# Layer norms: totals over partitions as columns of a product with one column of ones

## The reference

```
x <- LayerNorm(ALPHA * x + gate * sublayer(x * (1 + scale) + shift))

def layer_norm(x, g, b):
    mu = xf.mean(-1, keepdims=True)
    var = jnp.square(xf - mu).mean(-1, keepdims=True)
    return ((xf - mu) * lax.rsqrt(var + LN_EPS) * g + b)
```

## Time and profile before

| | |
|---|---|
| median of 3 runs | 3970.11 us |
| the profiled execution | 3970.7 us |
| its span | 3968.9 us |
| mean granted TensorE clock | 0.954 |
| TensorE busy | 3631.7 us (92%) |
| DVE busy | 2469.6 us (62%) |
| ACT busy | 937.8 us (24%) |
| POOL busy | 1844.6 us (46%) |

### The profile page before, as it was taken

The page is one execution under the profiler, slowest core; times in us unless marked ns, Lnnn a source line. Parts: engine busy times, 40 slices in busy tenths (PEclk is TensorE's granted clock), DMA queues, the critical chain, the costliest instruction groups (busy, mean ns, idle before and its releaser), DMA issues.

```text
span 3968.9 us, 74547 instructions
## 1 busy us (share of the span) xinstructions
PE 3631.7 (92%) x31532; PEld 3416.5 (86%) x31532; DVE 2469.6 (62%) x3517; ACT 937.8 (24%) x1804; POOL 1844.6 (46%) x875
## 2 busy tenths in 40 slices
PE   8999999999889778888999994899999989999998
PEld 3877799999778678888999994799998777899997
DVE  5366678758784456655885668886677556632125
ACT  5422231001243245542310012300013322220011
POOL 1310146656355645535566552366554201356663
PEclk9999999999999888999999997899999999999999
DMA  8100024333234443322343331244332000122221
GB/s 317 62 12 17 17 81 149 133 117 122 68 136 170 142 88 93 84 54 95 106 144 126 124 101 40 80 138 138 112 116 69 27 17 17 43 70 75 75 75 53
DMA packets 224972, 367.60 MB, mean 93 GB/s; under 512 B 104544, under 2 KB 109472, under 8 KB 224544
## 3 DMA queue, kind: packets, MB, share of 16 engines
q1 hardware_dynamic: 169536, 255.08, 20.9%
q10 hardware_dynamic: 55136, 107.98, 7.8%
HBM read 326.47 MB, written 36.54 MB: 91 GB/s over the span
## 4 chain that ended last, share of the span: by engine, by line
PE 71%; DVE 16%; ACT 4%; issue 4%; DMA 1%; SPq 1%; ACTq 1%; POOL 0%; DVEq 0%; POOLq 0%; PEldq 0%
PE ps L789 52%; PE ps L1061 3%; PE ps L1037 3%; DVE f_acc L2082 2%; PE ps L832 2%; PE ps L1047 2%; DVE m_mx L2313 1%; PE ps L1016 1%; DVE x L2180 1%; PE ps L997 1%; DVE x L2189 1%; DVE r_hlo L2364 1%; DVE ps L2531 1%; PE ps L849 1%; DVE s_T L2530 1%
## 5 line engine op out<-in xcount | busy, mean ns | idle before, releaser
L645 POOL TENSOR_TENSOR w_hi<-w_raw,zrow 128x1024 fp32r<-128x1024 f32 x354 | 697.0, 1969 | 1786.1 <-PE ps L789 992.6
L647 POOL TENSOR_TENSOR w_lo<-w_raw,w_hi 128x1024 fp32r<-128x1024 f32 x354 | 900.9, 2545 | 27.8
L2082 DVE SCALAR_TENSOR_TENSOR f_acc<-f_unit,silu_c,f_acc 128x512 f32<-128x512 f32 x504 | 631.3, 1293 | 7.6
L789 PE MATMUL ps<-f_hhi,w_hi 128*128 128x320 f32 x2688 | 633.9, 317 | 0.0
L789 PE MATMUL ps<-f_hhi,w_lo 128*128 128x320 f32 x2688 | 613.2, 309 | 0.0
L789 PE MATMUL ps<-f_hlo,w_hi 128*128 128x320 f32 x2688 | 610.7, 308 | 0.0
L789 PEld LDWEIGHTS ps<-f_hlo,w_hi 128*128 128x128 f32 x2688 | 449.9, 188 | 0.0
L789 PEld LDWEIGHTS ps<-f_hhi,w_lo 128*128 128x128 f32 x2688 | 448.8, 188 | 0.0
L789 PEld LDWEIGHTS ps<-f_hhi,w_hi 128*128 128x128 f32 x2688 | 441.2, 188 | 0.0
L789 PE MATMUL ps<-f_ahi,w_hi 128*128 128x320 f32 x1408 | 321.8, 310 | 0.2 <-DVE f_alo L2227 0.2
L789 PE MATMUL ps<-f_ahi,w_lo 128*128 128x320 f32 x1408 | 321.0, 309 | 0.0
(11 more groups left out here) (401 smaller groups left out, 6723.1 us busy)
## 6 DMA issues: line engine op xcount, KB each, us to landing
w_raw<-in_w SPq DMA_DIRECT2D x349, 512.0 KB, 3.5
f_unit<-in_ada_w ACTq DMA_DIRECT2D x72, 1024.0 KB, 5.8
ada_ring<-in_ada_w SPq DMA_DIRECT2D x24, 1024.0 KB, 6.3
up_scratch<-r_o ACTq DMA_DIRECT2D x40, 320.0 KB, 2.4
s_LW<-up_scratch SPq DMA_DIRECT2D x16, 320.0 KB, 4.9
s_LA<-up_scratch SPq DMA_DIRECT2D x8, 640.0 KB, 6.6
x<-in_x SPq DMA_DIRECT2D x1, 2560.0 KB, 10.0
x_scratch<-r_o ACTq DMA_DIRECT2D x8, 320.0 KB, 2.2
```

The lines of the kernel that those rows point to most:

```text
L645: nc.gpsimd.tensor_tensor(whi[:, slot, :], raw[:, raw_slot, :], zrow[:, 0:1].to_broadcast([P, CH * P]), ALU.add).then_inc(w_hi_done, 1)
L647: nc.gpsimd.tensor_tensor(wlo[:, slot, :], raw[:, raw_slot, :], whi[:, slot, :].bitcast(F32), ALU.subtract).then_inc(w_split, 1)
L789: last = mm(ps[:, 2 * b + h, 0:HT], w, r[:, h * HT:(h + 1) * HT], start=kt == 0 and n < 2, stop=kt == KT - 1 and n >= 4)
L2082: last = stt(acc[:, cd, :], unit[:, k, :], by, acc[:, cd, :], ALU.mult, ALU.add)
```

## The change

`turned` becomes `columns`: instead of five transposes of 128x128 it issues five products, each with a block of 128 tokens of the source as weights and one column of ones as the moving operand. Each gives the totals of 128 tokens as one column of PSUM, so a source gives five columns of one bank. DVE's four sums go: the small steps read these columns in PSUM where they lie. Three of its waits on itself go with them, and the semaphore `rd` with TensorE's wait for it. The totals lie in the banks 4, 5, 0 and 1, and the run-on ahead of the broadcast is on pair 1 instead of pair 2. Its six products, and all that comes after it, are as before.

```diff
-            def turned(t, src, b):
-
-                out = ps[:, 2 * b:2 * b + 2, :].rearrange("p b c -> p (b c)")
+            def columns(t, src, bank):
+
                 for j in range(NCH):
-                    last = nc.tensor.transpose(out[:, j * P:(j + 1) * P], src[:, j * P:(j + 1) * P], ident)
+                    last = mm(ps[:, bank, j:j + 1], src[:, j * P:(j + 1) * P], ones[:, 0:1], start=True, stop=True)
                 last.then_inc(q_ln[t].tr, 1)
 
             def totals(t, upd, at):
@@
                 pe.wait_ge(q.sh, q.at.sh + KD - 2)
                 pe.wait_ge(q.acc, q.at.acc + 1)
-                turned(t, m.S[:, 0, :], 2)
+                columns(t, m.S[:, 0, :], 4)
                 pe.wait_ge(q.acc, q.at.acc + 2)
-                turned(t, m.S[:, 1, :], 3)
+                columns(t, m.S[:, 1, :], 5)
                 pe.wait_ge(upd, at + KD)
-                turned(t, x[:, KD - 1, :], 0)
+                columns(t, x[:, KD - 1, :], 0)
                 pe.wait_ge(q.sq, q.at.sq + KD)
-                turned(t, m.S[:, 3, :], 1)
-                pe.wait_ge(q.rd, q.at.rd + 1)
-                run_on(2)
+                columns(t, m.S[:, 3, :], 1)
+                run_on(1)
@@
-                def total(n, b):
+                def total(n, bank):
                     dve.wait_ge(q.tr, q.at.tr + n)
-                    src = ps[:, 2 * b:2 * b + 2, :].rearrange("p b c -> p (b c)")[:, 0:T].rearrange("p (j t) -> p j t", j=NCH)
-                    return nc.vector.tensor_reduce(cols[:, n, :], src, AX.X, ALU.add)
+                    return ps[:, bank, 0:NCH]
@@
-                total(1, 2).then_inc(q.rd, 1)
-                dve.wait_ge(q.rd, q.at.rd + 1)
-                ch(total(2, 3))
-                ts(cols[:, 1, :], cols[:, 1, :], -1.0 / D, None, ALU.mult)
-                ch(ts(cols[:, 2, :], cols[:, 2, :], 1.0 / D, None, ALU.mult))
-                ch(total(3, 0))
-                ch(stt(cols[:, 0, :], cols[:, 3, :], -1.0 / D, cols[:, 1, :], ALU.mult, ALU.add))
-                ch(total(4, 1))
+                ts(cols[:, 1, :], total(1, 4), -1.0 / D, None, ALU.mult)
+                ch(ts(cols[:, 2, :], total(2, 5), 1.0 / D, None, ALU.mult))
+                ch(stt(cols[:, 0, :], total(3, 0), -1.0 / D, cols[:, 1, :], ALU.mult, ALU.add))
                 ch(tt(cols[:, 1, :], cols[:, 0, :], cols[:, 0, :], ALU.mult))
                 ch(tt(cols[:, 2, :], cols[:, 2, :], cols[:, 1, :], ALU.subtract))
-                stt(cols[:, 5, :], cols[:, 4, :], 1.0 / D, cols[:, 2, :], ALU.mult, ALU.add).then_inc(q.var, 1)
+                stt(cols[:, 5, :], total(4, 1), 1.0 / D, cols[:, 2, :], ALU.mult, ALU.add).then_inc(q.var, 1)
```

More of the change, by code:

```diff
@@ L421, in build @@
         q_split = dict(zip(splits, uses("split", dict(val=KD, hi=KD, lo=KD), len(splits))))
-        q_ln = uses("ln", dict(ksum=1, d=2, sh=KD - 2, sq=KD, cp=2, red=4, acc=2, tr=4, rd=1, var=1, sd=1, diag=2, bc=2, cen=KD, nrm=KD), 2 * DEPTH)
+        q_ln = uses("ln", dict(ksum=1, d=2, sh=KD - 2, sq=KD, cp=2, red=4, acc=2, tr=4, var=1, sd=1, diag=2, bc=2, cen=KD, nrm=KD), 2 * DEPTH)
         ln_fin = sem("ln_fin")
```

## The result

| | before | after |
|---|---|---|
| median of 4 runs each | 3971.09 us | 3999.61 us |
| lowest to highest | 3965.35 to 3973.65 | 3992.22 to 4002.74 |
| ratio, 95% interval | | 1.0082 (1.0067 to 1.0097) |
| span of the profiled execution | 3968.9 us | 4000.9 us |
| mean granted TensorE clock | 0.954 | 0.946 |

A fourth run of the kernel before has moved its median from 3970.11 to 3971.09 us. The changed kernel is 28.5 us slower by the medians, while DVE has 26.1 us less to do. The page of the changed kernel shows the shift in one line: the chain that ended last has more of TensorE (77% for 71%) and less of DVE (11% for 16%).

The account below looks back on a forecast made before the run. TensorE was taken as busy 92%, with DVE mattering only at the norms, where TensorE's strand was 0.63 us behind. Six norms 20.3, the fourth 3.1, the fifth 6.4: 29.8 us added, 4000 us, range 3976 to 4009.

Parts of the forecast that it names:

- Records and pace: TensorE in each norm: 40 records of column products at 0.111 us, 4.44 us, in place of 20 transpose records.
- The run-on in front of the broadcast: Six norms: run-on starts 1.61 us later and is ahead of the broadcast, so DVE starts 0.88 us later.
- The idle 0.63 us: TensorE's wait between run-on and broadcast in a norm before the change; said to decide the case.
- The clock: Narrow products make TensorE's clock fall in the norms; 1.7 to 3.4 us lost, middle 2.5 us a norm.
- L812's 3.1: Earlier long stretch of narrow products, where TensorE fell to 1.2 GHz about 3.1 us after it began; taken as guide.
- The fifth norm: Norm behind the pooling mixer, starting at low clock: products 4.3 us later, run-on 5.3 for 3.2 us; together 6.4.
- Sum: All eight norms: six 20.3 us together, the fourth 3.1, the fifth 6.4; 29.8 us added.
- the variance step comes over 1 us earlier: Sign in each norm: DVE's variance step over 1 us earlier with its sums gone, yet the addition to x later.
- The panels' own time: Projection panels outside the norms: nothing should change their time; the forecast is wrong if it changes.
- Rival 1: Clock holds in the norms, only the later run-on is paid: 8.1 us together, 3978 us; chance 0.15.
- Rival 2: A norm's products go as single records at a transpose's price: 5.4 us faster, 3964.7 us; chance 0.06.
- Rival 3: DVE's 26 us or part of it gained in the norms, needing the run-on out of the way; no own chance given.

Follow-up runs that it names:

- e1: Changed kernel with 100 equal columns of ones in each column product instead of 1: 3979.32 us, 1.0030 of the kernel before.
- e7: Kernel before with a first run-on of 10 products instead of 6: 3977.25 us, 1.0031 of the kernel before.
- e8: Kernel before with a first run-on of 7 products instead of 6: 3963.34 us in 1 run.
- e2: Changed kernel without the six run-on products between the columns and the broadcast: 3979.74 us, 1.0036 of the kernel before.
- e6: Changed kernel with 100 columns of ones and a run-on of 2 products instead of 6: 3959.62 us, 0.9991 of the kernel before.
- e4: Changed kernel, but S[0], S[1] by transposes and DVE sums, the rest by 100-column products, run-on of 2: 3949.36 us, 0.9954 of the kernel before.

## Why the prediction was right

It forecast 4000 us from 29.8 us of added time. Step by step:
- **Records and pace.** 40 records at 0.111 us: in the three norms whose products keep the clock the run-on starts 4.38 us after the first product (1056.55 - 1052.17), 4.44 forecast. A column step that reads PSUM takes 0.16 us, 0.2 assumed, off the path.
- **The run-on in front of the broadcast**, 0.88 us a norm at full clock: 0.89 in e1. The idle 0.63 us as the hinge: e7 and e8.
- **The clock, 2.5 us a norm as a middle of 1.7 and 3.4.** It fell in all seven norms; three of the six like ones lost 1.7 (low for 3.4 us) and three 3.3 (low for 6.8), which is 2.5 on the mean. That the mean came out at the middle is in part luck: e2 has the same products ahead of the run-on and other places of the fall. In the fourth norm it was the shorter (2.3 in place of 3.1 in all). The falls came 2.5 to 3.1 us after the first product in three norms and later in four; L812's 3.1 was near the early end.
- **The fifth norm:** 6.8 in place of 6.4, since the clock came back 5.0 us after the run-on's start and not 4.2. The forecast has a slip here: 40 x 0.21 is 8.4 and not 8.5, and then its own sum for this norm is 6.2. The run-on started 8.55 us after the first product, as the slip had it, since a record took 0.213.
- Sum 20.4 (forecast 20.3) in six norms, 2.3 (3.1) in the fourth, 6.8 (6.4) in the fifth: 29.4. The terms that missed, -0.8 and +0.4, partly cancel.
- **Wrong:** "the variance step comes over 1 us earlier". It does in three norms (4.63 us after the start; 5.74 before, 6.06 in the fourth). In the third it is 0.9 earlier (4.85), in three it is up to 0.6 us later, for their products ran partly at half rate, and in the fifth 2.9 later (8.81, 5.95 before). Nothing hung on it.
- **The panels' own time** should not change. 2.6 us lie outside the norms; that is within what runs of one kernel differ by, so it is neither shown nor excluded.
- **Rival 1** (the clock holds) had forecast 8.1 us: e1 shows this case, with 8.5. What it doubted is answered: 128 rows of weights in place of 2 do not hold the clock. It also counts the row of L849 wrongly: these are 16 records, so 8 products, in 1.84 us. **Rival 2** (a single record) is excluded by 320 records of L865 for 160 products. **Rival 3** (the sums' time gained) needs the run-on out of the way, as said, and the wide form too. Even so e6's norms gain 6.0 us and e4's 13.0, not 26, since the variance step then waits for TensorE's columns (0.55 us in e6, 0.19 in e4).

The Trainium skill, TensorE: Matmul & The Clock Gate, Part 4: PE-mode transpose, says that transposes do not count as busy for the clock. In the fifth norm of the kernel before TensorE had idled 12.7 us and then ran nothing but f32 transposes from 2506.49 to 2510.76, and the clock rose from 0.50 to 1.00 at their end. So the measurement decides against it for f32 transposes.

## What to carry to other kernels

Before taking work off the engine that the chain of waits names, measure how far the other strand is behind. Here it was 0.63 us of the 6.7 up to the broadcast. So with the run-on left as it was at most 0.7 us of the 3.3 us of sums could be gained, and the strand behind was the one that got the added work. Filler that keeps a clock is free only while something else takes its time: when that something is shortened, the filler has to be shortened with it. For f32 products with 128x128 weights one column of ones was no cheaper than a hundred, and cost 20.9 us more by the clock.

## What the runs showed of the hardware that was not expected

- A product of f32 with 100 columns keeps the pace of one with 1 column: 20 records in 2.37 and 2.29 us, both 0.11 apart. Up to there the columns are free. The weight loads are busy without a gap in both (4.30 of 4.30 us in e1, 2.70 of 2.70 here), so that they set the pace is likely, but no run varied them.
- A fall needs no idle time: neither the records of the products nor those of their weight loads leave a gap in any of the eight norms, and the clock went from 2.4 to 1.2 GHz in all seven that started at 2.4, 2.5 us in at the soonest (eighth norm; 2.1 in the fourth of e2).
- At the low clock the narrow products hold it down: 8.5 us of them in the fifth norm passed at 0.50, where transposes had brought it to 1.00 after 4.2 us.
